# A hybrid decoder step: five tiles of tokens through all experts in place of five and a half, one more tile by fetched rows

## What is computed

```
q = (ht @ w_query).reshape(T, 8, 2, 128)            # 8 heads, two half keys
s = einsum('thpd,hpnd->thpn', q, sub_keys)           # 128 scores a half key
top_s, top_i = top_k(s, 16)                          # 16 of each half
cand_s = top_s[:, :, 0, :, None] + top_s[:, :, 1, None, :]
fin_s, pos = top_k(cand_s, 16)                       # 16 experts a head, 128 a token
gate = softmax(fin_s)
act = gelu(einsum('tkd,td->tk', expert_u[idx], x))
out = einsum('tk,tkd->td', gate * act, expert_v[idx])
```

## Time and profile before

| | us |
|---|---|
| median of 3 runs | 3222.41 (3219.22 to 3223.44) |
| the profiled execution | 3221.37 |
| its span | 3219.6 |
| PE busy | 3107.1 |
| DVE busy | 2569.2 |
| ACT busy | 883.4 |
| POOL busy | 1126.0 |
| moved by DMA | 754.88 MB, 234 GB/s over the span |

### The profile page before, as it was taken

How to read it: one execution, slowest core, us unless ns; L and a number is a source line. 1 busy time by engine, 2 the same in 40 slices (tenths; PEclk the granted TensorE clock), 3 DMA queues, 4 the chain that set the end, 5 groups by cost and what they waited for, 6 DMA issues and landing times. The chain is left out here.

```text
span 3219.6 us, 45871 instructions
## 1 busy us (share of the span) xinstructions
PE 3107.1 (97%) x17420; PEld 2726.2 (85%) x17420; DVE 2569.2 (80%) x5687; ACT 883.4 (27%) x1307; POOL 1126.0 (35%) x758
## 2 busy tenths in 40 slices
PE   8999989899999999999999999998999999999998
PEld 7867765499999999999999999987777777777776
DVE  6621244357799999989888988858999999999996
ACT  4210300132122222224444444422222222222222
POOL 0000000000032222223333333324555886688881
PEclk9999989999999999999999999999999999999999
DMA  3010021351187777768888889899999999999993
GB/s 103 15 41 29 14 88 51 99 163 55 49 264 246 246 243 245 243 209 287 294 286 325 288 292 325 285 331 339 343 344 343 336 347 350 339 344 346 347 347 138
DMA packets 359908, 754.88 MB, mean 234 GB/s; under 512 B 37085, under 2 KB 205881, under 8 KB 354041
## 3 DMA queue, kind: packets, MB, share of 16 engines
q0 software_dynamic: 102576, 373.47, 34.3%
q1 hardware_dynamic: 257112, 378.49, 34.0%
HBM read 647.21 MB, written 102.25 MB: 233 GB/s over the span
## 5 line engine op out<-in xcount | busy, mean ns | idle before, releaser
L1931 POOL DMA_INDIRECT lead<-in_peer_v_dram,chosen x212 | 424.2, 2001 | 179.1 <-DVE acc_s L1950 128.1
L1931 POOL DMA_INDIRECT gr_row<-in_peer_u_dram,chosen x205 | 229.8, 1121 | 462.0 <-DVE chosen L1940 454.5
L1907 ACT ACTIVATE up_a<-up_pa 128x352 f32<-128x352 f32 x256 | 118.9, 464 | 755.3 <-PE up_pa L1892 662.5
L1931 POOL DMA_INDIRECT dr_row<-in_peer_v_dram,chosen x140 | 282.6, 2019 | 99.9 <-DVE acc_s L1950 72.4
L2694 DVE TENSOR_TENSOR acc<-pd_po,acc 128x512 f32<-128x512 f32 x384 | 278.7, 726 | 25.5 <-PE pd_po L2761 22.6
L1931 POOL DMA_INDIRECT s_sb<-in_peer_u_dram,chosen x147 | 159.3, 1084 | 374.7 <-DVE chosen L1940 369.1
L1950 DVE SCALAR_TENSOR_TENSOR acc_s<-lead,chosen,acc_s 128x1024 f32<-128x1024 f32 x212 | 279.9, 1320 | 0.0
L2340 ACT ACTIVATE lo_wx<-room 128x704 fp32r<-128x704 f32 x128 | 101.6, 794 | 623.6 <-DVE room L2331 623.6
L1940 DVE CUSTOM_DVE_ANT_0 gr_row<-gr_row,xs 128x1024 f32<-128x1024 f32 x205 | 248.6, 1220 | 14.4 <-DMA gr_row<-in_peer_u_dram,chosen 14.4
L511 PE MATMUL fr_a<-pj_w,h_t 128*128 128x256 f32 (+1 forms) x864 | 199.3, 393 | 0.9 <-PEq L186 0.9
L2462 DVE TENSOR_SCALAR pg_hot_i<-pg_iota,sel_t 128x128 f32<-128x128 f32 x704 | 195.7, 358 | 0.0
(11 more groups left out here) (484 smaller groups left out, 7420.1 us busy)
## 6 DMA issues: line engine op xcount, KB each, us to landing
lead<-in_peer_u_dram SPq DMA_DIRECT2D x128, 512.0 KB
room<-in_peer_v_dram SPq DMA_DIRECT2D x128, 512.0 KB
act_d<-up_a SPq DMA_DIRECT2D x256, 176.0 KB
room<-w_d SPq DMA_DIRECT2D x64, 704.0 KB, 6.6
room<-act_d SPq DMA_DIRECT2D x64, 704.0 KB
w_d<-pg_wb SPq DMA_DIRECT2D x24, 1024.0 KB, 7.0
w_d<-room SPq DMA_DIRECT2D x20, 1024.0 KB
lead<-in_peer_wq_dram SPq DMA_DIRECT2D x20, 512.0 KB, 3.9
```

The costliest lines, as they stand in the source:

```text
L1907: self.nc.scalar.activation(self.a_sb[c][:], self.pa[c][:, 0:WB], ACT.Gelu_apprx_tanh).then_inc(self.a_act, 1)
L1931: pool.indirect_dma_start(self.buf[i % self.n], None, self.table, bass.IndirectOffsetOnAxis(ap=self.idx[:, col:col + 1], axis=0)).then_inc ...
```

## The change

Dense are now five whole tiles, 640 tokens (`WB` = 320), sparse are three whole tiles and the 32 samples: `COLS` = 3 x 128 + 32 = 416. The packed slot holds the samples alone. The choice stage takes 17 U columns a tile, 119 in all, the gates stage the other 297; its groups are 160. The down stage has 10 slots a group (`OUTS`), all of 4 x 3 products, whose 12 makes are spread over 10 slots; `low_w` is one operation of 640 columns. The queries of the sparse tokens are 416 columns wide. The weights of the queries have three landing rooms in place of four for the first 16. The first two choices are of slots 5 and 6, and the packed copies come after block 21, when two choices are done.

```
-ORDER = (2, 3, 4, 5, 6, 7, 0, 1, 7)
-HALF_P = P // 2
-LAST = P - HALF_P + TS
-HEIGHTS = (P,) * 5 + (HALF_P, P, P, LAST)
-FIRSTS = tuple(ORDER[s] * P + (HALF_P if s == NT - 1 else 0) for s in range(NT))
-ND = 6
-TD = sum(HEIGHTS[:ND])
-NSP = 2
-TSP = NSP * P + LAST
+ORDER = (3, 4, 5, 6, 7, 0, 1, 2, 8)
+ND = 5
+TD = ND * P
+NSP = 3
+TSP = NSP * P + TS
 WB = TD // 2
-NB3 = (WB, WB, TSP)
-
-PACKS = ((0, P - HALF_P), (P - HALF_P, TS))
-NXS = NSP + len(PACKS)
-PACKED = sum(P // n for _, n in PACKS)
-PACK_AT = (NSP * NSEL, NSP * NSEL + PACKS[0][1])
-COLS = NSP * NSEL + LAST
+NXS = NSP + 1
+COLS = NSP * NSEL + NSEL // 4
+
+PACK = P // TS
...
-VISITS = (6, 7, 0, 8, 1, 2, 3, 4, 5)
+VISITS = (5, 6, 7, 8, 0, 1, 2, 3, 4)
...
-            return b % 4 if b < NU else (4 if b % 2 == 0 else 0)
+            return b % 3 if b < NU else (3, 4, 0)[(b - NU) % 3]
...
-            sp.wait_ge(rooted, 1)
-            sp.dma_start(rstd_last[0:P - HALF_P], rstd[HALF_P:P, NTP - 1:NTP]).then_inc(moved, 16)
-            sp.dma_start(rstd_last[P - HALF_P:LAST], rstd[0:TS, NTP:NT]).then_inc(moved, 16)
...
-                    mm = nc.tensor.matmul(pq[at % 3][:, 0:WB], w[b % 2][x][:, k, :], moving,
+                    mm = nc.tensor.matmul(pq[at % 3][:, 0:wide_of(b)], w[b % 2][x][:, k, :], moving,
...
-FIRST_CHOICE = (6, 7)
-CHOICE = (8, 0, 1, 2, 3, 4, 5)
+FIRST_CHOICE = (5, 6)
+CHOICE = (7, 8, 0, 1, 2, 3, 4)
...
-ROWS_A_TILE = 21
+ROWS_A_TILE = 17
...
-                if n == A_TILE + 3:
-                    sp.wait_ge(choice.chosen, 1)
-                    for i, own, source_own in packs():
-                        cols = slice(PACK_AT[i], PACK_AT[i] + PACKS[i][1])
-                        sp.dma_start(idx[own, cols], choice.idx_s[source_own, own]).then_inc(packed, 16)
-                        sp.dma_start(gate[own, cols], choice.gate_s[source_own, own]).then_inc(packed, 16)
-            sp.wait_ge(packed, 16 * 2 * PACKED)
+                if n == 2 * A_TILE + 3:
+                    sp.wait_ge(choice.chosen, choice.sparse)
+                    for own in packs():
+                        sp.dma_start(idx[own, NSP * NSEL:], choice.idx_s[0:TS, own]).then_inc(packed, 16)
+                        sp.dma_start(gate[own, NSP * NSEL:], choice.gate_s[0:TS, own]).then_inc(packed, 16)
+            sp.wait_ge(packed, 16 * 2 * PACK)
...
-        self.nc.vector.tensor_tensor(wx[:, NCH:NCH + 1], w[:, NCH - 1:NCH], wx[:, NCH - 1:NCH].bitcast(F32), ALU.subtract)
-        self.nc.vector.tensor_tensor(wx[:, NCH + 1:], w[:, 0:NCH - 1], wx[:, 0:NCH - 1].bitcast(F32), ALU.subtract
-                                     ).then_inc(self.w_lo, 1)
+        self.nc.vector.tensor_tensor(wx[:, NCH:], w, wx[:, 0:NCH].bitcast(F32), ALU.subtract).then_inc(self.w_lo, 1)
...
-OUT_SLOTS = (ND - 1,) + tuple(range(ND - 1))
+MAKES = 3 * GE
...
-FINAL = tuple(range(ND, NT)) + (ND - 1,) + tuple(range(ND - 1))
-FOLD_AT = 3
-INVERSE_AFTER = {0: (0,), 1: (1,), 2: (2,), 5: (3,), 6: (4,), 7: (5,), 9: (6,), 11: (7,)}
+FINAL = tuple(range(ND, NT)) + tuple(range(ND))
+INVERSE_AFTER = {0: (0,), 1: (1,), 2: (2,), 3: (3,), 4: (4,), 5: (5,), 7: (6,), 9: (7,)}
...
-                    m = GE * (g + 1) + o // 3
                     if g == 0:
                         add(g, o)
-                    if m < NK:
-                        (lower.multiply, lower.low_v, lower.low_w)[o % 3](dve, m)
+                    if g + 1 < NG:
+                        for i in range(MAKES * o // OUTS, MAKES * (o + 1) // OUTS):
+                            (lower.multiply, lower.low_v, lower.low_w)[i % 3](dve, GE * (g + 1) + i // 3)
                     if g >= 1:
                         add(g, o)
...
-                parts = ((0, None), (1, None)) if s == ND - 1 else PARTS
-                for x, y in parts:
+                for x, y in PARTS:
```

More of the change, by code:

```diff
@@ L1561, in _ @@
             load_w(2)
-            load_w(3)
             for i in range(NX + 1, NT):
                 load_x(i)
-                load_w(i - 1)
-            for i, own, source_own in packs():
[L1567 to L1570, removed]
+                load_w(i - 2)
+            sp.wait_ge(normed, VISITS.index(NT - 1) + 1)
+            for own in packs():
+                sp.dma_start(xs[own, NSP, :], x_pack).then_inc(packed, 16)
+            for b in range(NT - 2, 2 * NU):
                 load_w(b)
[L1572 to L1575, removed]
+            sp.wait_ge(w_lo, 2 * NU - 2)
+            up.load(sp, 1)
+            sp.wait_ge(w_lo, 2 * NU)
             up.load(sp, 0)
-            sp.wait_ge(packed, 16 * PACKED)
+            sp.wait_ge(packed, 16 * PACK)
         @block.gpsimd
@@ L2563, in peer_down @@
         pf = up.pa
-        gain, sq, x_s = rows_v.buf[0], rows_v.buf[1], rows_v.buf[2][0:LAST]
-        fold = [raw[:, i * LAST:(i + 1) * LAST] for i in range(len(PACKS))]
-        ss, rinv, rstd = (raw[:, len(PACKS) * LAST + i * NT:len(PACKS) * LAST + (i + 1) * NT] for i in range(3))
+        gain, sq, x_s = rows_v.buf[0], rows_v.buf[1], rows_v.buf[2][0:TS]
+        fold = raw[:, 0:TS]
+        ss, rinv, rstd = (raw[:, TS + i * NT:TS + (i + 1) * NT] for i in range(3))
         acc_in = [sem(f"acc_in{s}") for s in range(ND)]
-        accs_in, accs_zero, half_zero = sem("accs_in"), sem("accs_zero"), sem("half_zero")
+        accs_in, accs_zero = sem("accs_in"), sem("accs_zero")
         gain_loaded, zeroed, shaped, folded, taken = (sem(n) for n in ("gain_loaded", "zeroed", "shaped", "folded", "taken"))
@@ L2610, in _ @@
             sp.wait_ge(accs_zero, 1)
-            for i, (first, n) in enumerate(PACKS):
-                sp.dma_start(acc_s[0:n, NSP + i, :], x2_tiles[NT - 1][first:first + n]).then_inc(accs_in, 16)
+            sp.dma_start(acc_s[0:TS, NSP, :], x2_tiles[NT - 1]).then_inc(accs_in, 16)
             for m in range(2 * GE, NK):
@@ L2712, in take_samples @@
                     dve.wait_ge(folded, half + 1)
-                    nc.vector.tensor_copy(x_s[:, half * W4:(half + 1) * W4], pf[half][0:LAST, :]).then_inc(taken, 1)
+                    nc.vector.tensor_copy(x_s[:, half * W4:(half + 1) * W4], pf[half][0:TS, :]).then_inc(taken, 1)
                 dve.wait_ge(gain_loaded, 16)
-            def take_half():
-                for half in range(2):
-                    dve.wait_ge(folded, 3 + half)
-                    nc.vector.tensor_copy(acc[0:HALF_P, ND - 1, half * W4:(half + 1) * W4], pf[half][0:HALF_P, :]).then_inc(taken, 1)
             for m in range(1, GE):
@@ L2777, in _ @@
                 if g == NG - 1:
-                    pe.wait_ge(shaped, PACKED)
+                    pe.wait_ge(shaped, PACK)
                     pe.wait_ge(rows_v.used, COLS)
                     for half in range(2):
-                        for i in range(len(PACKS)):
-                            mm = nc.tensor.matmul(pf[half][0:LAST, :], fold[i][:], acc_s[:, NSP + i, half * W4:(half + 1) * W4],
-                                                  start=(i == 0), stop=(i == len(PACKS) - 1))
-                        mm.then_inc(folded, 1)
+                        nc.tensor.matmul(pf[half][0:TS, :], fold, acc_s[:, NSP, half * W4:(half + 1) * W4],
+                                         start=True, stop=True).then_inc(folded, 1)
                 for o in range(NPO if g == 0 else 0, OUTS):
                     at = OUTS * g + o
-                    if g == NG - 1 and o == FOLD_AT:
-                        pe.wait_ge(taken, 2)
-                        pe.wait_ge(o_added, OUTS * g + 2)
-                        for half in range(2):
-                            nc.tensor.matmul(pf[half][0:HALF_P, :], fold[0][:, 0:HALF_P], acc[:, ND - 1, half * W4:(half + 1) * W4],
-                                             start=True, stop=True).then_inc(folded, 1)
                     if at >= NPO:
```

132 lines of the change are left out of this document (53 added, 79 removed).

## The result

The changed kernel takes 3343.45 us (median of 4 runs, 3337.3 to 3345.5), the kernel before, run beside it, 3222.55: ratio 1.0374, 95% interval 1.0356 to 1.0392. Slower, as forecast; the forecast was 3314, so 29 us too low and inside the range. The profiled execution took 3342.4 us (span 3340.3), 121.0 more than that of before.

The account below looks back on a forecast made before the run. PE was taken to bound the choice and gates stages, DVE the down stage. From the profiled 3221.4 us, -38 (choice), +38 (gates) and +93 (down) gave +93, about 3314 us, range 3220 to 3375.

Parts of the forecast that it names:

- Scores: Scores stage: product columns added and taken away are the same number, so 0 us, with 5 us kept either way.
- Choice: Choice stage, 64 blocks: narrower products save 41 us, 3 us kept for bumps, sum -38 us (bounds -41 and -20).
- Gates: Gates stage and last blocks: DVE becomes the bound (-9 and -4), late fetches add +31 and 20; sum +38 us.
- late fetches: Gates stage: U row fetches late where DMA engines are full, +31 us, and 20 in the last six blocks; bounds 0, +112.
- Down: Down stage: 8 DVE work, 20 dependent rows, 58 waiting for PE, 5 gathers, 3 and -1 small; sum +93 us.
- the wait at the first add: Down stage: PE restarts at low clock into a 12-product slot; DVE waits 2.0 us in each of 29 groups, +58.
- Adjacent rows: Down stage: in 126 slots with two rows the second waits about 0.16 us for the first's write, +20 us.
- PE restarting in time: Down groups: first slot ready within 2.9 us of PE's start and fetches in time, 3200 us; chance 0.13.
- Only the clock term missing: Whole kernel: DVE and fetches as computed, but no low-clock cost in the down stage, 3256 us; chance 0.14.
- The DMA engines: Down stage: DMA engines bound at 342 GB/s, 37.7 us a group with the cold wait, 3351 us; chance 0.10.
- GpSimd only at adds: Down stage: fetches get through only at DVE's adds, so DVE stands for 4.3 a group, +135, 3449 us; chance 0.07.
- rival 4: Down stage: GpSimd held up by DVE's two-input operations, its fetches passing only at adds, 3449 us; chance 0.07.

Follow-up runs that it names:

- before_early: Kernel before the change, with a down group's 12 makes in eleven of its twelve slots: 3220.2 us, ratio 0.9994.
- makes_early: Changed kernel, with the twelve makes of a down group in nine of its ten slots: 3276.65 us.
- rows_apart2: Changed kernel, where a down slot has two rows, the first put behind the slot's first make so that they are not adjacent: 3317.45 us.
- filler24: Changed kernel, with 24 unused products of 128 columns on PE behind each down group: 3297.3 us.
- half_loads: Changed kernel, with later plain loads of U and V bringing only the left half of each row, 66 MB less: 3324.6 us.
- combo20_apart: Changed kernel with five row buffers, makes over nine slots, 20 choice columns a tile and a slot's rows apart: 3201.0 us, ratio 0.9933 to the kernel before.

## Why the prediction was right, and where its sizes were off

**Scores, 0 with 5 either way:** +4.6, within it. The changed kernels range from +0.7 to +7.1 there, and before_early, whose scores stage is that of the kernel before, has +4.8: this is the spread of the stage, no more.

**Choice, -38:** -43.2 for 60 blocks, 5 us more than forecast and past the bound of -41. A block went from 8.65 to 7.93 us; the forecast had 8.6 and 7.97, and the 3 us kept for bumps were not needed. Products start 0.147 us apart (1.17 for eight), as foretold. That DVE would keep up held: 457.3 of 470.

**Gates, +38:** +62.1, the term that was mis-sized. Its parts were a floor by DVE (-13) and late fetches (+51). The waits of dots for fetches rose from 14.4 to 92.2, +78, and the rest is -16. So the floor was right and the fetch term 27 us too small. The mis-sized step: "I take a third of the 269 rows of the first 58 blocks at 2.7", each late by 0.34 us, +31. The picture of stretches in which the DMA engines are full was right, and they are those behind the writes of the gate matrix. But a row that is late there is late by more than its pace: 41 dots in the blocks between the entry and the last batch waited over 0.3 us, 59 us together, 1.4 us each. A fifth buffer rides over part of it and gives back 34 us in the stage. The last blocks, forecast at 20, have 24 with the tenth batch. Blocks took 12.3 us on average, above the 11.1 to 11.8 foretold, and DVE was at 91% (631 of 693), not near 100%. The bound taken for the fetches, 112, held.

**Down, +93:** +97.2. By parts: the wait at the first add, +58 forecast, 59.6 measured, and 58 given back by makes_early; the first slot took 4.1 to 5.3 us, the forecast had 4.3 to 5.4, and the stand was 7.1 for about 7. Adjacent rows, +20 at 0.16 each: 21 given back by rows_apart2 in this stage, at 0.19 a pair. (The row that the forecast cites, 1.31 us long for a distance of 1.19, gives 0.12; the 0.16 was a guess above it.) Late gathers, +5: 0.5 us of waits, not there. Rows, makes and adds, +10 with the small terms: what is left, 97 - 60 - 21 = 16. A group of 36.4 us was forecast and 36.6 came. The cause named, the low clock behind the stand, has at least 39 of these 58 us, as filler24 shows, and about 50 by the estimate there; the rest is that a slot of twelve products is late even at full clock when DVE comes after one row.

The four errors are +5, -5, +24 and +4. So little of the total is luck: it is 29 us low for the most part by the gates.

**Rivals.** PE restarting in time (3200) fell by the 59.6 us of waits. Only the clock term missing (3256) fell with it. The DMA engines (3351) gave nearly the right time, and for the wrong reason: half_loads took 29 GB/s from the down stage and it did not move, and makes_early carried 354 GB/s in it, above the 342 that this rival took as the limit. That case shows how a sum close to the measured one proves nothing. GpSimd only at adds (3449) fell too: in the kernel after, 374 fetches passed in 26 groups (2247 to 3200 us), which hold 260 adds, and DVE waited 0.5 us for fetches in all. The forecast's own account of how they pass, openings between adjacent rows, is wrong: rows_apart2 has none of them and fetches are faster still, 1.35 us for 1.48. The Trainium skill (GPSIMD Engine Reference, Key points) names contention of this engine with VectorE's instructions of two SBUF inputs. That there is contention agrees: in the kernel after, a fetch took 1.10 us in the choice stage (123.51/112) and 1.48 in the down stage, where rows, low parts and products with the gates all read two inputs from SBUF. That it would wait for each of them to be over, as rival 4 took the rule, no run bears out. What lets a fetch through between two different two-input operations stays open.

## What to carry to other kernels

When an engine loses work but not its place in the chain, ask how long it will now stand in each turn of the loop and what it restarts with: here 11% less work for TensorE, with more rows for VectorE, turned a stand of 1.7 us into 7.1, with a low clock behind it and 2 us a group for the engine that was the bound. The cheap cure is to finish what it waits for one slot earlier, which cost nothing where it wasn't needed (before_early, 3220.2 for 3221.1). And where a reader waits for gathers, look when it waits before taking a mean pace: here it was behind bursts of writes, and one more buffer bridged part of them.

## What was not expected of the hardware

- Work without a use on the waiting engine paid: 24 products of 5.5 us in a stand of 7.1 took the kernel from 3343 to 3297 us, 50 of them, 11.3 us, to 3389. The 24 didn't keep the clock up in every group: in eight it fell all the same.
- A fetch by GpSimd cost 2.02 us in the down stage before, 1.48 after and 1.35 with the rows apart. In the kernel before, VectorE never paused, and each of the 330 fetches from 2247 to 3200 us ended 0.9 us behind the start of an add. Pauses alone don't explain the difference: in combo20_apart VectorE is busy 927 of 953 us, with 12 adjacent pairs of rows for 113, and a fetch takes 1.38 us (522.77/378). What frees them in the kernels after was not settled.
- DMA engines that read 0.94 busy were no bound: with 0.90 the stage took the same time, and with 0.97 (makes_early) less.
